# Stage ends by semaphores alone, gate columns behind the placement, and two PSUM banks cleared by VectorE

## The reference

```python
def hierarchical_moe(h, ...):                       # h: 1024 tokens x 1024
    g_top, g_idx = top_k(softmax(h @ w_group + b_group), 1)       # one of 4 groups
    e_top, e_idx = top_k(logits of the 8 experts of that group, 2)
    weights = g_top * softmax(e_top)
    # each token goes to 2 of 32 experts:
    #   hid = silu(x @ w_gate[e]) * (x @ w_up[e]);  y = hid @ w_down[e]     (1024 -> 512 -> 1024)
    return sum over its two experts of weight * y
x = layer_norm(ALPHA * x + (1 + gt_f) * y)
```

## Time and profile before

| what | us |
|---|---|
| median of 3 runs | 3562.01 (3561.36 to 3571.13) |
| the profiled execution | 3574.29 |
| its span, first to last instruction | 3572.6 |
| TensorE busy in it | 3199.2 (90%) |
| experts, layer 0 | 1163 to 1757 |
| experts, layer 1 | 2926 to 3504 |

### The profile page before, as it was taken

One profiled execution on the slowest core, in us unless ns is written; L12 is line 12 of the kernel. 1 busy time (PEld: TensorE's weight loads), 2 busy tenths in 40 slices (PEclk: granted clock), 3 DMA queues, 4 the chain that ended last, 5 costly groups with the idle time before them and its releaser, 6 DMA issues. The chain is left out here.

```text
span 3572.6 us, 42657 instructions
## 1 busy us (share of the span) xinstructions
PE 3199.2 (90%) x15005; PEld 1742.4 (49%) x15006; DVE 1243.4 (35%) x3003; ACT 881.7 (25%) x1714; POOL 616.3 (17%) x1035
## 2 busy tenths in 40 slices
PE   8987979947796999999789999999989969988885
PEld 6665664437643344334356666666644434333332
DVE  5665554445434122212242223322322231122223
ACT  1022224313311111111034445544520011111111
POOL 0000000046411111212121111111110001122123
PEclk9888999957798999999899999999999979999998
DMA  7730001122134898998441111011031158899975
GB/s 293 265 113 4 0 12 30 42 58 57 41 122 192 333 368 354 412 397 355 182 169 36 36 36 36 3 34 36 1 126 36 36 228 322 335 426 423 409 302 205
DMA packets 181624, 612.92 MB, mean 172 GB/s; under 512 B 54637, under 2 KB 105544, under 8 KB 148462
## 3 DMA queue, kind: packets, MB, share of 16 engines
q1 hardware_dynamic: 159118, 566.97, 41.1%
q0 software_dynamic: 22080, 42.01, 3.1%
q10 hardware_dynamic: 288, 2.10, 0.2%
HBM read 592.59 MB, written 52.99 MB: 181 GB/s over the span
## 5 line engine op out<-in xcount | busy, mean ns | idle before, releaser
L1897 PE MATMUL ret_pqkv<-ret_w,hT_mix 128*128 128x512 f32 x1024 | 451.9, 594 | 2.6 <-PEq L2636 2.6
L2470 PE MATMUL f0e_pgu<-f0w_gu,f0e_xT 128*64 128x512 f32 x1568 | 344.4, 595 | 8.4 <-issue 4.6
L1759 PE MATMUL mo_py<-mo_w,mixT 128*128 128x512 f32 x768 | 336.8, 599 | 5.8 <-DMA mo_w<-in_ret_w_out_dram 3.1
L2470 PE MATMUL f1e_pgu<-f1w_gu,f1e_xT 128*64 128x512 f32 x1344 | 294.3, 592 | 8.8 <-issue 5.0
L1897 PEld LDWEIGHTS ret_pqkv<-ret_w,hT_mix 128*128 128x128 f32 x1024 | 190.3, 191 | 218.4 <-issue 218.3
L1759 PEld LDWEIGHTS mo_py<-mo_w,mixT 128*128 128x128 f32 x768 | 146.6, 192 | 188.7 <-issue 179.9
L2470 PEld LDWEIGHTS f0e_pgu<-f0w_gu,f0e_xT 128*64 128x64 f32 x1568 | 125.9, 137 | 221.3 <-issue 221.3
L1905 PE MATMUL ret_pgate<-ret_w,hT_mix 128*128 128x256 f32 x1024 | 231.6, 379 | 0.0
L2489 PE MATMUL f1e_pd<-f1w_d,f1e_hidT 128*64 128x512 f32 x672 | 168.3, 652 | 42.9 <-DMA f1w_d<-in_moe_w_down_dram 38.5
L1905 PEld LDWEIGHTS ret_pgate<-ret_w,hT_mix 128*128 128x128 f32 x1024 | 189.6, 190 | 23.6 <-issue 0.5
L2470 PEld LDWEIGHTS f1e_pgu<-f1w_gu,f1e_xT 128*64 128x64 f32 x1344 | 103.7, 137 | 194.2 <-issue 194.2
(11 more groups left out here) (566 smaller groups left out, 4736.0 us busy)
## 6 DMA issues: line engine op xcount, KB each, us to landing
f0w_gu<-in_moe_w_gate_dram SPq DMA_DIRECT2D x32, 2048.0 KB
f0w_gu<-in_moe_w_up_dram SPq DMA_DIRECT2D x32, 2048.0 KB
f0w_d<-in_moe_w_down_dram SPq DMA_DIRECT2D x64, 1024.0 KB
f1w_gu<-in_moe_w_gate_dram SPq DMA_DIRECT2D x32, 2048.0 KB
f1w_gu<-in_moe_w_up_dram SPq DMA_DIRECT2D x32, 2048.0 KB
f1w_d<-in_moe_w_down_dram SPq DMA_DIRECT2D x64, 1024.0 KB
mixT<-in_ada_w_dram SPq DMA_DIRECT2D x80, 512.0 KB, 5.6
ret_w<-in_ret_w_in_dram SPq DMA_DIRECT2D x16, 1024.0 KB, 10.0
```

The lines of the kernel that those rows point to most:

```text
L1759: mm = pe.matmul(py[t % 3][:, half * 512:(half + 1) * 512], mixT[:, kk, t * P:(t + 1) * P], ws[:, kk, half * 512:(half + 1) * 512], start= ...
L1897: mm = pe.matmul(p_qkv[s % 2][:, :], g.hT[:, kk, t * P:(t + 1) * P], w[h % 2][:, kk, 0:512], start=(kk == 0), stop=(kk == KD - 1))
L2470: mm = pe.matmul(pgu[s][half * HALF:(half + 1) * HALF, :], xT[u % 2][:, kk, s * HALF:(s + 1) * HALF], ew.gu[u][:, :, kk, half * FH:(half + ...
```

## The change

In `route`, TensorE's two matmuls for the gate columns, with their wait for ScalarE's tiles, stand behind the 16 placing matmuls. In `experts`, the two banks are set to zero by VectorE at the start of its list, and TensorE waits for that (`cleared`) after its first `turn`; the two matmuls are gone.

```diff
--- before.py
+++ after.py
@@ -113,7 +113,7 @@
             self.stages += 1
 
         ctx.callback(ended)
-        return ctx.enter_context(self.nc.Block())
+        return ctx.enter_context(self.nc.Block(no_gpsimd_drain=True))
 
 
 
@@ -2154,22 +2154,22 @@
 
         @block.tensor
         def _(pe):
+            pe.wait_ge(S["onehot"], 1)
+            pe.matmul(pr[:, 0:NT * NE], g.before[:, :], C[:, :, 1:NT + 1], start=True, stop=False)
+            pe.matmul(pr[:, 0:NT * NE], g.ones[:, :], Cp[:, :, 0:NT], start=False, stop=True)
+            pe.matmul(pr[:, NT * NE:(NT + 1) * NE], g.ones[:, :], Cp[:, :, NT], start=True, stop=True)\
+                .then_inc(S["ranked"], 1)
+
+            for n in range(2 * NT):
+                pe.wait_ge(S["hit"], n + 2)
+                pe.matmul(pkT[:, :], B[:, n % 2, n // 2, :], A[n % NH][:, :], start=(n == 0), stop=(n == 2 * NT - 1))\
+                    .then_inc(S["placed"], 1)
             pe.wait_ge(S["diagd"], 1)
             for c in range(2):
                 mm = pe.matmul(pgate[c * 64:c * 64 + 64, :], g.ones[:, 0:64], diag[:, 4 * c:4 * c + 4, :], start=True,
                                stop=True, skip_group_check=True)
             mm.then_inc(S["gated"], 1)
 
-            pe.wait_ge(S["onehot"], 1)
-            pe.matmul(pr[:, 0:NT * NE], g.before[:, :], C[:, :, 1:NT + 1], start=True, stop=False)
-            pe.matmul(pr[:, 0:NT * NE], g.ones[:, :], Cp[:, :, 0:NT], start=False, stop=True)
-            pe.matmul(pr[:, NT * NE:(NT + 1) * NE], g.ones[:, :], Cp[:, :, NT], start=True, stop=True)\
-                .then_inc(S["ranked"], 1)
-
-            for n in range(2 * NT):
-                pe.wait_ge(S["hit"], n + 2)
-                pe.matmul(pkT[:, :], B[:, n % 2, n // 2, :], A[n % NH][:, :], start=(n == 0), stop=(n == 2 * NT - 1))\
-                    .then_inc(S["placed"], 1)
             pe.wait_ge(S["copied"], 1)
             pe.transpose(pk[:, 0:NBLK], pairT[:, :], g.ident[0:NBLK, 0:NBLK]).then_inc(S["turned"], 1)
 
@@ -2352,7 +2352,7 @@
         ph = g.ps(ctx, f"{tag}_ph", [P, 512])
         pd = [g.ps(ctx, f"{tag}_pd{s}", [P, 512]) for s in range(2)]
 
-        names = "xt_a xt_b xa xd gu_a gu_b silu_a silu_b hid_a hid_b ht hTd down_a down_b ya yb asked left".split()
+        names = "xt_a xt_b xa xd gu_a gu_b silu_a silu_b hid_a hid_b ht hTd down_a down_b ya yb asked left cleared".split()
         S = dict(zip(names, g.sems(ctx, tag, *names)))
 
         pairs = {n: g.sems(ctx, tag, n + "0", n + "1") for n in "idxd didxd stored".split()}
@@ -2518,9 +2518,8 @@
             def is_full(m, u):
                 return pe.value_load(full[0:1, bass.ds(m, 1), u], min_val=0, max_val=1)
 
-            for bank in (pgu[1], pd[1]):
-                pe.matmul(bank[:, :], g.ident[:, :], g.cos[:, 0:8, :].rearrange("p t n -> p (t n)"), start=True, stop=True)
             turn(0, 0)
+            pe.wait_ge(S["cleared"], 2)
             second = [is_full(0, u) for u in range(QUAD)]
             for u in range(QUAD):
                 gates(0, u, second[u])
@@ -2608,6 +2607,8 @@
                     dve.wait_ge(S[down], m * QUAD + (u + 1))
                     dve.tensor_tensor(y[b][:, s, :], pd[s][:, :], r.gate[:, :], ALU.mult).then_inc(S[done], 1)
 
+            for bank in (pgu[1], pd[1]):
+                dve.memset(bank[:, :], 0.0).then_inc(S["cleared"], 1)
             take(0, 0)
             for u in range(QUAD):
                 if u:
```

More of the change, by code:

```diff
@@ L2156, in _ @@
         def _(pe):
[L2157 to L2161, removed]
             pe.wait_ge(S["onehot"], 1)
@@ L2172, in _ @@
                     .then_inc(S["placed"], 1)
+            pe.wait_ge(S["diagd"], 1)
+            for c in range(2):
+                mm = pe.matmul(pgate[c * 64:c * 64 + 64, :], g.ones[:, 0:64], diag[:, 4 * c:4 * c + 4, :], start=True,
+                               stop=True, skip_group_check=True)
+            mm.then_inc(S["gated"], 1)
             pe.wait_ge(S["copied"], 1)
```

## The result

The changed kernel took 3546.93 us (median of 8 runs, 3539.46 to 3551.11) beside 3565.97 us for the kernel before on the same chip. The ratio is 0.9942, with a 95% interval of 0.9929 to 0.9956: 20.7 us less, between 15.7 and 25.3 (the two medians differ by 19.0). The forecast was 21.7 less. Its time, 3540.3 us, started from a median of only three runs, 3562.01; with eight runs the kernel before stands at 3565.97, so the measured time lies 6.6 us above the forecast one and at the very edge of the narrower range, 3534 to 3547, though the gain is nearly the one forecast. The profiled execution has a span of 3545.4 us instead of 3572.6, but part of those 27 us is luck: routing in layer 0 began 4.6 us earlier than before, ahead of any stage that the sum prices.

A forecast was written before the change was run, and what follows sets the result against it. TensorE, busy 90% of the span, bounds the kernel, so only its standstills can go. Route to gates 7.9, experts' ends 13.0, combine's ends 0.6 and 0.2 sum to 21.7 us: 3562.01 to 3540.3, range 3534 to 3547 (wider 3529 to 3552).

The forecast's parts named there:

- Gate columns: In route, moving the gate matmuls behind the placement frees VectorE earlier: net 5.5 us per layer, bounds 5.0 and 6.0.
- The gather: End of route: the first gather, beside full weight loads, taken to need 10.5 us, ends 6.2 and 11.3.
- From barrier to gates: End of route to the experts' first gates: gates begin 6.3 us (layer 0) and 6.0 us (layer 1) earlier, before clock loss.
- The clock: Experts' first gates begin at 1.2 GHz without TensorE's fills: 2.2 us lost per layer, 1.7 to 2.7 or perhaps nothing.
- The ends of experts: Pause after the last scatter shrinks by 6.6 us in layer 0 and 6.4 us in layer 1, sum 13.0.
- The ends of combine: Barrier wait shrinks: 0.6 us in layer 0 (bounds 0 and 0.9), 0.2 at the last combine (0 and 0.6).
- nine other ends: Stage ends where another engine is last: nothing won, to within 0.1 us each.
- Layer 1's loads: Layer 1 experts: load stream moves up, whole gain counted; more down-weight waiting than 38.5 us would show it wrong.
- GpSimd's reset behind the barrier: Start of the experts stage: GpSimd's own drains may wait for the gathers until about 1160, costing nothing.
- rival 2: GpSimd's place in the barrier still waits for its queue: 4.9 us of gain left, 3557 us; chance 0.05.
- Rival 1: End of route: gathers aren't slowed and the clock rises early, 9 to 13 us more, 3529 us; chance 0.20.
- Rivals 3 and 4: Low clock through first block's gates, 3557 us, chance 0.05; through the second block's too, 3585 us, chance 0.03.

The follow-up runs named there:

- e2: Kernel before with only the gate columns moved behind the placement, drains and TensorE's bank fills kept: 3570.11 us, ratio 1.0016.
- e8: Changed kernel with SyncE asking for the third and fourth slots' weights only once the first gather has landed: 3530.66 us, ratio 0.9895.
- e6: Changed kernel with the banks filled once by TensorE ahead of its first turn instead of cleared by VectorE: 3547.41 us, one run.
- e7: Changed kernel with the banks filled four times over by TensorE ahead of its first turn instead of cleared by VectorE: 3544.73 us, ratio 0.9934.
- e11: Changed kernel with third and fourth slots' loads held until the first gather landed and banks filled once by TensorE: 3532.96 us, ratio 0.9902.
- e4: Changed kernel with GpSimd's drain put back at the ends of the two experts stages alone: 3560.55 us, ratio 0.9988.
- e3: Kernel before with only the two banks cleared by VectorE instead of TensorE, drains and gate order kept: 3567.06 us, ratio 1.0008.
- e9: Changed kernel with third and fourth slots' loads held until the first gather landed and banks filled twice over by TensorE: 3535.77 us, ratio 0.9912.
- e10: Kernel before with third and fourth slots' loads held until the first gather landed, drains, order and fills kept: 3568.33 us, one run.

## Why the prediction held

The mechanism was right in its main steps: what each barrier waited for, that the gather is late next, that it slows beside the loads, and that the first gates pay with the clock. The size is right partly because misses cancel. In the terms of the sum:

- Gate columns, 5.5 us per layer, bounds 5.0 and 6.0. The gather was issued 31.4 and 32.0 us after the stage's start, and is now issued after 25.6 and 25.4: 5.9 and 6.6, in layer 1 past the bound. But e2 shows that this edit wins nothing by itself. The prediction didn't see that: it priced the edits in one line, as if each had a value of its own.
- The gather, taken at 10.5 us between 6.2 and 11.3. Measured 10.8 and 11.7, in layer 1 past the slow bound, where it takes back what the earlier issue gives: +1.1 and -1.0 us, luck for the sum. e8 shows the cause, by taking it away. The Trainium skill (DMA: Bandwidth & Descriptors, "Queues, rings and completion order") has each DMA engine take turns between its queues by packets; by itself that didn't keep the gather from taking more than twice its 4.6 us, and the row of the loaded gather was the better guide.
- From barrier to gates, 6.3 and 6.0 us; measured in A 6.5 and 6.1. That VectorE's clearing brings part of this was wrong: e6 has the fills back on TensorE and an A of 39.2 and 40.6, as the early barrier moves them into a wait.
- The clock, 2.2 us per layer, bounds 1.7 to 2.7; measured 2.7 and 2.2. It rose about 5.5 and 4.5 us after the first gate matmul, 9.0 and 8.0 after the first transpose; before, it rose 3.3 and 5.4 us after the first fill. The Trainium skill (TensorE: Matmul & The Clock Gate, "Part 4: PE-mode transpose") says that transposes don't count; the trace agrees, as the distance from the first gate matmul is like the one from the first fill in the earlier trace rows, and the one from the first transpose is not. In e7 and e11, with TensorE busy up to the landing, B loses nothing, but the second block's gates do.
- The ends of experts, 13.0 us. Measured 6.4 + 6.6 = 13.0, and e4 takes exactly that back.
- The ends of combine, 0.6 and 0.2 us. The stage's length doesn't show them (layer 0 took 71.3 us before and 72.8 and 72.0 in the two profiles after, layer 1 67.5 and 66.3 and 68.1), but its end does: in layer 0 TensorE's pause is 0.6 us shorter. In layer 1, from the last store's issue to the end of the span, it is 4.4 us instead of 5.2, so about 0.9, above the bound of 0.6. Of the nine other ends, at which I expected no change beyond 0.1 us, eight cost 0.05 to 0.07 us more from the last engine's work to the barrier, and that of the attention stage 0.35 more (0.20 before, 0.55 after, by the semaphore records). None of this is in "parts".
- Layer 1's loads. TensorE's waits for down weights came to 41.2 us instead of 38.5, the sign that I had named as one against me. The sign was badly chosen: they are 40.8 in e2 and 41.0 in e3, which win nothing, and C didn't grow.
- GpSimd's reset behind the barrier, which was to last until about 1160, began with a drain of 1.3 us, which ended with the issue of the second gather: it doesn't wait for gathers in flight. Neither did the barrier, so rival 2 is out.

A, B and D sum to 20.7 us, as the first group of runs measured; the second gave 16.8, so an agreement this close is luck too. Rival 1 (gathers not slowed) is out, since they were. The time that it priced was there all the same, for whoever holds the loads back: e8 is 16 us faster than the changed kernel. Rivals 3 and 4 are out, since the clock rose within the first block's gates.

What stays open: the parts of the other kernels overshoot their measured gain by up to 9 us. The dips in the second block's gates explain 3.4 us of it in e7 and in e11 and 1.7 in e9. For the rest the profiles show no stage in which it is lost again. It may be the granted clock elsewhere in the kernel, as the attention stage's 10 us suggest, or the scatter of the times, but no run isolates it.

## What to carry to other kernels

Edits around one barrier don't add: here the drain's removal lost 5 us at the end of routing, the gate columns alone and the banks alone won nothing, and the three together won 7.7 us there (by A and B). Price such a group by asking what is latest after each subset. When a barrier goes and the next thing late is a small transfer, look at what is loading beside it and hold back what isn't needed yet: that gave 16 us here. Filling TensorE's remaining wait with dense matmuls that end when the data lands made the first gates run at full clock, but no measured time shows a gain from it.

## What the runs showed of the hardware

- GpSimd's two gathers (126 rows of 4 KB in layer 0, 141 in layer 1, so 0.52 and 0.58 MB for both together) are issued 1.5 us apart. The first took 4.4 to 4.6 us from its issue to its landing with the loads held back (e8, e9, e10, e11; in e8 the queues moved 240 GB/s in all meanwhile), and 10.5 to 11.8 where the queues moved 427 GB/s in all; the second then took up to 16.4. The Trainium skill (DMA: Bandwidth & Descriptors, "Anatomy of one DMA — SWDGE (gpsimd) path") fits 2.0 us plus the bytes at 436 per ns: even for 128 full rows, the most that one gather can move, that is an estimate of 3.2 us; the runs say 4.4 at least.
- The drain of GpSimd's queue at the end of the experts stages kept the barrier shut for 6.4 us (layer 0) and 6.6 us (layer 1) longer than waiting for the scatters by semaphore does. At the end of routing with held loads it opened 0.3 us after the second gather had landed (e10). Why the same drain has a long tail behind scatters and none behind gathers isn't settled.
- After 6.06 us of standing still (e6, layer 0), in which the clock fell from 2.4 to 1.2 GHz, the turn took 1.97 us; after 0.65 us (e7) it took 1.15, at 2.4.
- With the first gates at full clock throughout, the clock fell to half for 3.4 us in the second block's gates in six stages of twelve, and these gates took 15.6 to 15.7 us instead of 13.95.
